# Two-layer block plus mixer block in one launch: weight parts interleaved in the networks, moving columns of rounded products read from last to first

## What is computed

```python
def swiglu_layer(x, norm_g, w_gate_up, w_down):          # hidden width 2816
    h = rmsnorm(x, norm_g)
    g, u = jnp.split(h @ w_gate_up, 2, axis=-1)
    return x + (jax.nn.silu(g) * u) @ w_down

# first block: x -> recurrent layer (w_in, w_out) -> network -> attention layer (w_qkv, w_out) -> network
# second block, twice: h @ w_in (18 projections), latent attention, RWKV and GLA branches,
#                      merged @ w_out, all products float32
```

## Time and profile before

| | |
|---|---|
| median of the runs | 1950.8 us |
| profiled execution, its own time | 1952.72 us |
| its span, first to last instruction | 1950.9 us |
| granted TensorE clock, mean of the span | 0.994 |
| PE busy | 1868.4 us, 96% |
| DVE busy | 1339.9 us, 69% |
| ACT busy | 746.9 us, 38% |
| PE share of the chain that ended last | 78% |

### The profile page before, as it was taken

One profiled execution on the slowest core, in us unless ns is written; L12 is line 12 of the kernel. 1 busy time (PEld: TensorE's weight loads), 2 busy tenths in 40 slices (PEclk: granted clock), 3 DMA queues, 4 the chain that ended last, 5 costly groups with the idle time before them and its releaser, 6 DMA issues.

```text
span 1950.9 us, 42020 instructions
## 1 busy us (share of the span) xinstructions
PE 1868.4 (96%) x18191; PEld 1733.3 (89%) x18191; DVE 1339.9 (69%) x1755; ACT 746.9 (38%) x1099; POOL 88.9 (5%) x131
## 2 busy tenths in 40 slices
PE   7999999999899999999999999998999999999999
PEld 7987999998699999988887899897998887889988
DVE  8896678757648876864576469666764766458755
ACT  5572533444533342231235233254213233325154
POOL 2000000000400000011000000000002000000000
PEclk9999999999999999999999999998999999999999
DMA  8554477964347785654540145553663542035644
GB/s 222 141 152 150 134 254 259 276 189 129 99 134 259 253 258 135 168 146 116 143 130 15 52 117 172 134 159 108 171 177 87 152 130 57 25 99 162 171 116 137
DMA packets 473225, 291.90 MB, mean 150 GB/s; under 512 B 26775, under 2 KB 467580, under 8 KB 472872
## 3 DMA queue, kind: packets, MB, share of 16 engines
q1 hardware_dynamic: 466720, 262.13, 48.1%
q0 software_dynamic: 5312, 25.32, 3.4%
q10 hardware_dynamic: 1032, 2.11, 0.5%
HBM read 287.95 MB, written 1.05 MB: 148 GB/s over the span
## 4 chain that ended last, share of the span: by engine, by line
PE 78%; DVE 13%; ACT 4%; issue 2%; DMA 2%; ACTq 0%; POOL 0%; DVEq 0%; SPq 0%
PE bank L709 39%; PE bank L1487 6%; PE bank L1489 5%; PE bank L1488 5%; DVE rounded L734 3%; PE bank L668 3%; PE bank L950 3%; PE bank L698 2%; PE bank L1693 1%; PE bank L1680 1%; PE bank L1117 1%; ACT rounded L723 1%; DVE rounded L718 1%; PE bank L791 1%; PE bank L942 1%
## 5 line engine op out<-in xcount | busy, mean ns | idle before, releaser
L709 PE MATMUL bank<-rounded 128*128 128x256 f32 (+1 forms) x5160 | 622.6, 281 | 10.7 <-DVE rounded L734 8.6
L709 PEld LDWEIGHTS bank<-rounded 128*128 128x128 f32 (+1 forms) x5160 | 608.0, 186 | 20.7 <-DVE rounded L734 12.4
L734 DVE TENSOR_TENSOR rounded<-arena,rounded 128x1024 fp32r<-128x1024 f32 (+1 forms) x275 | 331.8, 1214 | 77.0 <-ACT rounded L723 69.5
L1487 PE MATMUL bank<-parts 128*128 128x256 f32 x1024 | 286.9, 280 | 1.8 <-DVE parts L2314 1.7
L1489 PE MATMUL bank<-parts 128*128 128x256 f32 x1024 | 285.8, 279 | 0.0
L1488 PE MATMUL bank<-parts 128*128 128x256 f32 x1024 | 285.6, 279 | 0.0
L774 ACT ACTIVATE arena<-bank 128x512 f32<-128x512 f32 x114 | 67.7, 597 | 351.9 <-PE bank L709 339.5
L709 PE MATMUL bank<-common,arena 128*128 128x256 f32 x896 | 199.4, 380 | 0.0
L723 ACT ACTIVATE rounded<-arena 128x1024 fp32r<-128x1024 f32 x144 | 150.5, 1055 | 116.6 <-PE bank L709 72.9
L1487 PEld LDWEIGHTS bank<-parts 128*128 128x128 f32 x1024 | 192.4, 188 | 2.9 <-issue 1.6
L1489 PEld LDWEIGHTS bank<-parts 128*128 128x128 f32 x1024 | 193.0, 188 | 0.0
(11 more groups left out here) (409 smaller groups left out, 2396.1 us busy)
## 6 DMA issues: line engine op xcount, KB each, us to landing
arena<-in_w_in SPq DMA_DIRECT2D x190, 512.0 KB, 3.8
whole<-in_ffn_w_gate_up SPq DMA_DIRECT2D x44, 1024.0 KB, 5.2
arena<-in_ada_w POOLq DMA_DIRECT2D x32, 768.0 KB, 6.6
whole<-in_ffn_w_down SPq DMA_DIRECT2D x16, 1408.0 KB, 7.2
arena<-in_rec_w_in SPq DMA_DIRECT2D x36, 512.0 KB, 3.8
arena<-in_att_w_qkv SPq DMA_DIRECT2D x24, 512.0 KB, 4.0
arena<-in_rec_w_out SPq DMA_DIRECT2D x16, 512.0 KB, 4.0
arena<-in_mla_w_o SPq DMA_DIRECT2D x16, 512.0 KB, 4.1
```

The lines of the kernel that those rows point to most:

```text
L709: last = pe.matmul(psum[s][0:c, m % 2 * T:m % 2 * T + T], w[a][:, k, cols], x[b][:, k, :], start=(k, a, b) == (0, 0, 0), stop=k == job.kt ...
L734: dve.tensor_tensor(raw_view(job_of[u], u, UNIT_LOW), raw, high_view(job_of[u], u).bitcast(F32), ALU.subtract)\
L1487: pe.matmul(bank, w_hi, x_hi, start=start and k == 0, stop=False)
```

## The change

Three things are edited. The high and low weight parts of a slot of the networks are interleaved element by element in the same memory, so that each is read and written with a step of two floats. In every rounded product the moving operand, and the bank that it is written to, is given as a view with step minus one, so that the columns go through from the last to the first and land where they did. In the two networks and in the attention layer's products `H_SHIFT` goes from 16 to 32 floats and `HIDDEN_SHIFT` from 48 to 32. `X_SHIFT` stays.

```diff
-        X_SHIFT, H_SHIFT, HIDDEN_SHIFT = (16, 16), (16, 16), (48, 48)
+        X_SHIFT, H_SHIFT, HIDDEN_SHIFT = (16, 16), (32, 32), (32, 32)
...
-        part_slots = [[parts[:, (2 * s + e) * slot_floats:(2 * s + e + 1) * slot_floats] for e in range(2)] for s in range(2)]
+        part_pairs = [parts[:, 2 * s * slot_floats:(2 * s + 2) * slot_floats].rearrange("p (n e) -> p e n", e=2) for s in range(2)]
+        part_slots = [[pair[:, e, :] for e in range(2)] for pair in part_pairs]
...
+        def backwards(x):
+
+            return x[:, ::-1]
...
-                            last = pe.matmul(psum[s][:, i * T:i * T + T], w[a][:, kk, :], job.rhs[b][:, kk, :],
+                            last = pe.matmul(backwards(psum[s][:, i * T:i * T + T]), w[a][:, kk, :], backwards(job.rhs[b][:, kk, :]),
...
+            order = backwards if job.high else lambda v: v
...
-                                last = pe.matmul(psum[s][:, t * COLS:t * COLS + COLS], x[b][:, at + k, t * P:t * P + P],
-                                                 w[a][:, k, n * COLS:n * COLS + COLS], start=begins, stop=ends, skip_group_check=True)
+                                last = pe.matmul(backwards(psum[s][:, t * COLS:t * COLS + COLS]), x[b][:, at + k, t * P:t * P + P],
+                                                 backwards(w[a][:, k, n * COLS:n * COLS + COLS]), start=begins, stop=ends, skip_group_check=True)
...
-                            last = pe.matmul(psum[s][0:c, m % 2 * T:m % 2 * T + T], w[a][:, k, cols], x[b][:, k, :],
+                            last = pe.matmul(order(psum[s][0:c, m % 2 * T:m % 2 * T + T]), w[a][:, k, cols], order(x[b][:, k, :]),
...
-                x_hi, x_lo = (e[:, k, :] for e in x)
+                x_hi, x_lo = (backwards(e[:, k, :]) for e in x)
...
-                    last = three_passes(psum[s][:, m * T:m * T + T], UP_W[s], slice(m * P, m * P + P), DK, H_PARTS, True, True)
+                    last = three_passes(backwards(psum[s][:, m * T:m * T + T]), UP_W[s], slice(m * P, m * P + P), DK, H_PARTS, True, True)
```

More of the change, by code:

```diff
@@ L1501, in ffn_pe @@
                         for kk in (k, k + 1):
-                            last = pe.matmul(psum[0][:, m * T:m * T + T], UP_W[0][a][:, kk, m * P:m * P + P], H_PARTS[b][:, kk, :],
+                            last = pe.matmul(backwards(psum[0][:, m * T:m * T + T]), UP_W[0][a][:, kk, m * P:m * P + P], backwards(H_PARTS[b][:, kk, :]),
                                              start=(m, kk, a, b) == (0, 0, 0, 0), stop=kk == DK - 1 and a == 1, skip_group_check=True)
@@ L1526, in ffn_pe @@
                     pe.wait_ge(lo_ready[0].sem, j * 2 + (turns + UPS + q + 1))
-                    three_passes(psum[q][:, 0:T], DOWN_W[0], slice(0, P), UPS, [x[:, 0:UPS] for x in HIDDEN_PARTS], True, False)\
+                    three_passes(backwards(psum[q][:, 0:T]), DOWN_W[0], slice(0, P), UPS, [x[:, 0:UPS] for x in HIDDEN_PARTS], True, False)\
                         .then_inc(first_part_used.sem, 1)
@@ L1530, in ffn_pe @@
                     pe.wait_ge(lo_ready[1].sem, j * 2 + (turns + UPS + q + 1))
-                    three_passes(psum[q][:, 0:T], DOWN_W[1], slice(0, P), UPS, [x[:, UPS:] for x in HIDDEN_PARTS], False, True)\
+                    three_passes(backwards(psum[q][:, 0:T]), DOWN_W[1], slice(0, P), UPS, [x[:, UPS:] for x in HIDDEN_PARTS], False, True)\
                         .then_inc(product[q].sem, 1)
```

## The result

The changed kernel takes 1970.0 us (median of five, 1967.83 to 1973.83) against 1956.5 us for the kernel before on the same chip (five runs, 1950.65 to 1963.39): ratio 1.0073, interval 1.005 to 1.0096. The forecast was 1923 us, with 1898 to 1967 as the range, so the time moved the other way: 13.5 us up, a small loss but clear of no change. In its profiled execution the span is 1966.5 us, 15.6 more than before.

The account below looks back on a forecast made before the run. PE's matmul pitch was taken as the bound. Gains of 11.4 us in the networks and 22.0 outside, 85% reaching the end, took 28.4 us off 1952.7; less 1.9 to the median, 1923 us, range 1898 to 1967.

Parts of the forecast that it names:

- What bounds the kernel: Whole kernel: PE busy 96% of the span and 78% of the last chain, so the pitch of its matmuls must move.
- two sharp pitches at a clock of 1.00: Same code in and outside the networks runs in long stretches at about 117.8 or 113.3 ns.
- The 85%: Share of the 33.4 us of saved PE time taken to reach the kernel's end: 28.4 us.
- a third pitch: Sign in the profile after that the forecast is wrong: rounded products at a pitch other than the two seen.
- Reversed moving columns and interleaved weights: All rounded products: both reads run the same way, pitch 113.3 ns; 11.4 us gained in the networks, 22.0 outside.
- the low pitch of the 16-column rows: Products with 16-column weights run at 114 ns, read as moving columns and weight loads getting in each other's way less.
- rival C: All rounded products: no gain, stalls perhaps set a phase by chance and address order doesn't enter; 1951 us, chance 0.17.
- Rival D: Rounded products: with X_SHIFT still 16 the two reads meet for longer; +16 us, 1967 us, chance 0.12.
- Strided splits: Networks' high parts on ScalarE and low parts on VectorE, with a step of two floats: costed at nothing.
- their cover: Networks' up turn of 96 matmuls, 11.3 us, hides the splits: DVE busy 83% or 9.4 us, ACT 38%.
- Shift constants: H_SHIFT also moves the attention layer's moving operand: 1 ns on some 600 matmuls, under 1 us.
- rival E: Strided splits slow the networks, up to +126 us, or reversed bank writes run at half rate, +820 us; chance 0.06.

Follow-up runs that it names:

- both runs of streams: Only streams of rounded products, none of the reference's layers: 48 kinds by direction, step, weight width and shift, then 23 forward kinds by distance; pitches 113.3 to 121.1 ns.
- the run of the networks alone: Kernel before with only the networks interleaved and reversed at shifts of 32, attention products forwards at 32: 1958.7 against 1955.0 us, ratio 1.0019.

## Why the prediction was wrong

*What bounds the kernel* held: the pitch is what moved, and the span followed it. Reading two sharp pitches at a clock of 1.00 was right as well. The 85% that was to reach the end was too much: about 63% did, as worked out above. It came from the share of line 709 in the chain over its busy time, which isn't a measure of how much of a saving gets through. The prediction's own sign of being wrong, a third pitch, is what came.

*The step that failed* is the one under "Reversed moving columns and interleaved weights": "The target is then the pitch without a conflict, 113.3 ns". It was put at -4.5 ns for the slow products and measured at +2.2 outside (117.8 to 120.0) and 0 in the networks, where also the low stretches were lost. Behind it stood two readings, and both broke. The reversed read has a cost of its own: narrow streams that read forwards fall to 113.5 ns and reversed ones never under 117.7, and with 128 columns none of the eight shifts reached the target either. And the low pitch of the 16-column rows was no proof that the two reads meet less there. In both runs of streams bursts with the full 128 columns reach 113.3 to 113.7 ns, and one narrow burst of three stood at 116.7. I took a state that a stretch falls into for a property of the operands. The prediction had the sign of it before it, the same code at both pitches, and kept it as rival C with a chance of 0.17; a second profile of the kernel before would have told.

The premise, that the weight load walks its block from the last column, and half as fast as the columns go through, stays unshown: no run gives the order of a single read. What the streams show is that the distance still matters with reversed columns and a step of two (120.0 ns at shift 0, 117.8 at 16 to 48).

*Rival D* (0.12) named place and size nearly: the old `X_SHIFT` under reversed columns, 1967 us, against 1970.0. The size is partly luck. It put 1.9 ns on all 9768 products from a row at 118.6 ns, where 2.5 ns on those outside and 0.9 in the networks were measured, and took 85% of it, from a start that was 4 to 6 us low. Its mechanism is borne out in part. At 48 the first long stretch comes down from 120.0 to 117.6 ns, and no further; the loss against 113.3 is the direction's.

*Strided splits* were costed at nothing. VectorE's were free (2292 to 2294 ns). ScalarE's were not: 1918 to 2165 ns, 13%, and 1380 to 1531, 11%. They stayed under their cover, which is shown by the idle time before the networks' matmuls, 1.8 us before and 1.7 after.

The Trainium skill (SBUF — State Buffer, section "Door 1") led to expect that two hits per 16-byte line are enough. For VectorE these rows agree; for ScalarE they don't.

*Shift constants.* The attention layer's products were given 1 ns on some 600. Forwards at shift 32 they cost 1.8 ns more, as the run of the networks alone shows, and 3.0 ns more in the changed kernel, reversed at the same shift (117.0 to 120.0 ns): 1 to 2 us, under the noise.

*The bank's direction* (in rival E) costs nothing, as the streams with the bank alone reversed show.

*The level of before.* The forecast started from a median of three, 1950.8 us. The medians of the later series are 1955.0, 1954.9 and 1956.4 us, and 1956.5 for five runs. So some 4 to 6 us of the distance between 1923 and 1970.0 is the start and not the change.

What stays open: why a reversed read costs some 4 ns against the low pitch, what at the start of a stretch picks the pitch, and why moving both operands by the same amount changes how often. No run here looks inside a single read.

## What to carry to other kernels

When one instruction runs at two sharp speeds in one trace, profile the same kernel again before explaining either by its operands: if the stretches swap, the better speed is something to make likelier, not a target to reach. A stream of one kind of matmul per source line puts fifty layouts into one run of a millisecond. Its table gave the pitch of the reversed and interleaved stretches shown here to within 0.3 ns. For forward reads, where a layout has two pitches, three bursts were too few: at shift 48 all three were low, and the kernel then had 117.8 as well. Two edits made for each other (here step and direction) are to be run one at a time too: in the networks the reversal only undid what the interleaving lost. And before a time is shared out by pitches, compare the granted clocks of the two profiles. Against the profile at 0.994 the share that reached the end was 83%, against the one at 0.991, nearer to the changed kernel's 0.990, it was 62%.

## What the hardware showed beside

Float32r matmuls of 256 columns have pitches of 113.3, 117.8 and 120.0 ns in most long stretches, by direction, step and distance, at a granted clock of 1.00; single layouts in the streams lie between (116.7, 118.4, 118.6). The duration in the profile doesn't name the pitch: it is 276 ns at 113.3, but at 117.8 it is 279 to 282, and 282 or 283 at 120.0. The weight load does bear on the running matmul: at shift 64 and forwards, 16 columns of weights give 113.5 ns in two of three bursts and 128 columns 119.9.

```profile
L64 PE MATMUL bank<-moving,weights 128*128 128x256 f32 x144 | 18.0, 285 | 0.0
...
L208 PE MATMUL bank<-moving,weights 128*16 128x256 f32 x144 | 17.0, 277 | 0.0
```

The Trainium skill (TensorE: Matmul & The Clock Gate, Part 2, step 1) has the two reads independent of each other; these two rows differ by 1.0 us in 144 matmuls, and the measurement decides. The narrow stream also writes 16 partitions of the bank and not 128, so the cleaner pair is that of the table at shift 48, forwards, where only the layout of the weights differs: 113.6 and 120.1 ns. The weight loads themselves last 195 ns instead of 188 with a step of two.
